# A tuned one-core transformer layer on Trainium2: 512 more columns of the projection in the opening sweep, a first softmax that stays unscaled, and modulation rows dealt out later

## The reference, cut to what matters

```python
ada = jax.nn.silu(c) @ w_ada[i] + b_ada[i]
sh_m, sc_m, gt_m, sh_f, sc_f, gt_f = [a[:, None, :] for a in jnp.split(ada, 6, axis=-1)]
h = rms_norm(x, g_pre_mix[i]) * (1 + sc_m) + sh_m
...
proj = h @ w_in
qa, ka, va, qb, kb, vb, rb, zb = jnp.split(proj, IN_SPLITS, axis=-1)
...
    p = jax.nn.softmax(s, axis=-1)
    pd = p[:, :, 0] - lam * p[:, :, 1]
    return jnp.einsum('bhqk,bhkd->bhqd', pd.astype(v.dtype), vt)
...
o = rms_norm(o, sub_gain) * (1.0 - lam_init)
```

## Time and profile before

| | |
|---|---|
| median of 3 runs | 1465.71 us (1464.82 to 1466.46) |
| the profiled execution | 1463.97 us, its span 1462.0 us |
| PE busy | 1221.2 us (84%) |
| DVE busy | 778.9 us (53%) |
| ACT, POOL busy | 211.7 us (14%), 52.9 us (4%) |
| DMA | 583.52 MB, mean 399 GB/s |

### The profile page before, as it was taken

The page is one execution under the profiler, slowest core; times in us unless marked ns, Lnnn a source line. Parts: engine busy times, 40 slices in busy tenths (PEclk is TensorE's granted clock), DMA queues, the critical chain, the costliest instruction groups (busy, mean ns, idle before and its releaser), DMA issues.

```text
span 1462.0 us, 18971 instructions
## 1 busy us (share of the span) xinstructions
PE 1221.2 (84%) x7437; PEld 575.1 (39%) x7438; DVE 778.9 (53%) x1110; ACT 211.7 (14%) x491; POOL 52.9 (4%) x68
## 2 busy tenths in 40 slices
PE   4699999999999989886777677758676679999967
PEld 4578884744444443222222222212222223333322
DVE  5877487877769666342234323422333335555525
ACT  3010121232110041010000000000000001111103
POOL 1000300011100020000000000000000000000020
PEclk9899999999999999988888889987888889999989
DMA  9999988797999899999999999999999999999996
GB/s 354 392 383 384 351 317 346 291 378 274 367 409 412 345 379 396 431 430 433 431 432 431 430 434 430 430 432 432 434 431 432 431 432 431 431 432 430 433 427 262
DMA packets 81557, 583.52 MB, mean 399 GB/s; under 512 B 5280, under 2 KB 30160, under 8 KB 56816
## 3 DMA queue, kind: packets, MB, share of 16 engines
q1 hardware_dynamic: 74160, 564.41, 93.6%
q10 hardware_dynamic: 5808, 14.85, 2.7%
q0 software_dynamic: 1552, 3.75, 0.8%
HBM read 579.30 MB, written 3.69 MB: 399 GB/s over the span
## 4 chain that ended last, share of the span: by engine, by line
PE 45%; DMA 44%; DVE 6%; SPq 2%; issue 1%; ACT 1%; POOL 0%; ACTq 0%; DVEq 0%
DMA stream<-in_w 41%; PE ps L1019 9%; PE ps L788 8%; PE ps L675 5%; PE ps L1075 4%; PE ps L740 3%; DMA stream<-in_w_ada 3%; PE ps L1026 2%; PE ps L975 2%; PE ps L878 2%; PE ps L969 2%; SPq L510 2%; PE ps L785 1%; DVE stream L1298 1%; DVE wk L1161 1%; DVE acc L1270 1%
## 5 line engine op out<-in xcount | busy, mean ns | idle before, releaser
L1019 PE MATMUL ps<-stream,wk 128*32 128x512 f32 x2304 | 330.2, 711 | 179.6 <-DMA stream<-in_w 178.9
L1536 DVE TENSOR_TENSOR acc<-ps,acc 128x2048 f32<-128x2048 f32 x37 | 84.8, 2292 | 364.4 <-PE ps L975 364.4
L1019 PEld LDWEIGHTS ps<-stream,wk 128*32 128x32 f32 x2304 | 74.7, 125 | 417.5 <-issue 332.5
L788 PE MATMUL ps<-stream 128*128 128x512 f32 x320 | 140.5, 593 | 0.1
L1075 PE MATMUL ps<-stream,cst 128*32 128x512 f32 x1152 | 131.5, 595 | 8.4 <-DMA stream<-in_w 8.4
L675 PE MATMUL ps<-stream 128*128 128x256 f32 x512 | 118.1, 394 | 1.8 <-ACT stream L1681 1.8
L675 PEld LDWEIGHTS ps<-stream 128*128 128x128 f32 x512 | 100.9, 198 | 16.8 <-issue 1.9
L1026 PEld LDWEIGHTS ps<-cst,wk 128*128 128x128 f32 x576 | 76.4, 207 | 69.0 <-issue 69.0
L975 PE MATMUL ps<-wk,cst 32*128 32x512 f32 x592 | 91.1, 687 | 0.8 <-ACT wk L1876 0.8
L1161 DVE SCALAR_TENSOR_TENSOR wk<-stream,cc,wk 128x768 f32<-128x768 f32 (+1 forms) x90 | 83.6, 929 | 11.0 <-DMA stream<-in_w_ada 8.3
L788 PEld LDWEIGHTS ps<-stream 128*128 128x128 f32 x320 | 59.5, 190 | 69.7 <-issue 69.7
(11 more groups left out here) (281 smaller groups left out, 1105.4 us busy)
## 6 DMA issues: line engine op xcount, KB each, us to landing
stream<-in_w SPq DMA_DIRECT2D x87, 4096.0 KB, 41.9
stream<-in_w_ada SPq DMA_DIRECT2D x64, 1024.0 KB, 8.8
stream<-in_w_in SPq DMA_DIRECT2D x8, 4096.0 KB, 16.5
stream<-in_w SPq DMA_DIRECT2D x16, 2048.0 KB, 11.7
stream<-in_w_ada SPq DMA_DIRECT2D x64, 384.0 KB, 10.1
stream<-in_w_ada SPq DMA_DIRECT2D x16, 512.0 KB, 9.7
stream<-in_w_in SPq DMA_DIRECT2D x4, 2048.0 KB, 13.7
stream<-in_w_out SPq DMA_DIRECT2D x2, 4096.0 KB, 16.4
```

The source lines that it names most:

```text
L788: last = nc.tensor.matmul(bank(fill % 2), hT[:, k, P * half:P * half + P], w[:, k, :], start=(k == 0), stop=(k == KD - 1))
L1019: last = nc.tensor.matmul(bank(1 + m)[32 * g:32 * g + 32, :], xe[:, k + g, :], w13[m][:, k + g, :], start=(k == 0), stop=(k == KD - 4))
L1536: V.tensor_tensor(y4, ps[:, b0:b0 + 4, :], y4, ALU.add).then_inc(ysum_sb, 1)
```

## The change

- **The opening sweep takes ten units.** `WIDE = 10`: units 8 and 9 are new. Each is the product of one tile of 128 positions with columns 2048 to 2559 of w_in (the first half of va), one matmul of 512 columns for each of the stage's rows. Their weights come as further slabs (`wide_slabs`, `wide_home`, L545 of the changed kernel), 2 KB a partition and row, 4.2 MB in all. Both share bank 6 with units 6 and 7, so there are four hand-overs of that bank in a stage where there were two (`SHARED = 4`, and `ADDED_AT` for their places on DVE; the fourth stands behind the stage's transposition and sum). `TURN = [6, 0, 7, 1, 8, 2, 3, 4, 9, 5]`.
- **The projection has 28 slots.** Block unit 4 is gone with its load, its 56 matmuls and its DVE sums; unit 5 is the only seven-product block. Plain projection starts in slot 4, attention too (`ATT_FROM = 4`).
- **`ADA_IN` is new.** In the last eight slots of the projection stand 18 of the 64 rows (3, 3, 3, 2, 1, 2, 2, 2 after an empty slot), where 16 stood in the last ten; two rows fewer (14) beside w_out.
- **The relative bias row** (L711 before) moves ahead of the sweep's last unit and into bank 7; its two tables are loaded on a semaphore of their own.
- **The first softmax stays unscaled.** L1414 is gone, and L1412 inverts one number in place of two. The two maps are combined as p0 + (l0/l1)(-lam) p1, where l0 and l1 are the softmax sums, and the RMS norm behind it absorbs the missing factor: POOL adds EPS * 128 * l0^2 to the sum of squares before the power. That adds two small operations a group of four steps on POOL ahead of its wait for the squares, and changes no count behind it.

The diff, cut to its core:

```diff
-HEADS_READY = [8, 16]
 EARLY = 8
+WIDE = 10
+SHARED = WIDE - 6
 HELD = 6
-TURN = [6, 0, 1, 2, 7, 3, 4, 5]
-SLOTS = 32
-BLOCK_UNITS = [4, 5]
+TURN = [6, 0, 7, 1, 8, 2, 3, 4, 9, 5]
+ADDED_AT = {8: {1: 6, 3: 7, 5: 8}, 4: {0: 6, 2: 7, 3: 8}}
+SLOTS = 28
+BLOCK_UNITS = [5]
-ATT_FROM = 6
-ADA_IN = [1, 1, 1, 1, 1, 1, 1, 1, 2, 2, 2, 2, 0, 2, 2, 1, 2, 2, 2, 1, 2, 2, 0, 2, 1, 2, 2, 2, 3, 2, 2, 0, 4, 5, 4, 3]
+ATT_FROM = 4
+ADA_IN = [1, 1, 1, 1, 2, 2, 2, 2, 2, 2, 0, 2, 2, 2, 2, 2, 2, 2, 2, 0, 3, 3, 3, 2, 1, 2, 2, 2, 4, 4, 3, 3]
...
+                for a_, b_ in wide_slabs(j):
+                    if a_ == 6:
+                        sp.wait_ge(xT_ps, 4 * TT)
+                    sp.dma_start(wide_home(a_, b_), w_in[:, a_:b_, 256 * EARLY:256 * EARLY + 512]).then_inc(early_w_in[j % 3], 16)
...
                 if not held and j + u > HELD:
-                    pe.wait_ge(add_sb, 2 * j + u - HELD)
+                    pe.wait_ge(add_sb, SHARED * j + u - HELD)
+                if u >= EARLY:
+                    t = u - EARLY
+                    for k in range(lo, hi):
+                        last = nc.tensor.matmul(bank(HELD), hT[:, k, P * t:P * t + P], wide_home(k, k + 1)[:, 0, :], start=(k == lo), stop=(k == hi - 1))
+                    last.then_inc(add_ps, 1)
+                    return last
...
+                    if n == WIDE - 1 and j + 1 == len(STAGES):
+                        pe.wait_ge(tab_in, 16 * len(tables))
+                        pe.wait_ge(early_mod, len(STAGES))
+                        nc.tensor.matmul(bank(7)[:, 0:SKEW], relb, bkt[:, 0:SKEW], start=True, stop=True).then_inc(relrow_ps, 1)
...
-                    if j and n_ in (len(pieces(j)) // 4, 3 * len(pieces(j)) // 4):
-                        added(j - 1, HELD + n_ // (len(pieces(j)) // 2))
+                    if j and n_ in ADDED_AT[len(pieces(j))]:
+                        added(j - 1, ADDED_AT[len(pieces(j))][n_])
...
+                if j:
+                    added(j - 1, WIDE - 1)
...
-                        link(V.reciprocal(st[:, 12:14], st[:, 10:12]))
-                        link(V.tensor_tensor(st[:, 14:15], st[:, 13:14], lamv[:, 5:6], ALU.mult))
-                        link(V.tensor_scalar(pr[:, 0, 0:nk], pr[:, 0, 0:nk], st[:, 12:13], None, ALU.mult))
+                        link(V.reciprocal(st[:, 13:14], st[:, 11:12]))
+                        link(V.scalar_tensor_tensor(out=st[:, 14:15], in0=st[:, 13:14], scalar=lamv[:, 5:6], in1=st[:, L0(i):L0(i) + 1], op0=ALU.mult, op1=ALU.mult))
...
+                    least = st[:, L0(4 * g):L0(4 * g) + 4]
+                    pool.wait_ge(p_exp, 4 * g + 4)
+                    pool.wait_ge(pd_sb, 4 * g + 4)
+                    link(nc.gpsimd.tensor_tensor(least, least, least, ALU.mult))
+                    link(nc.gpsimd.tensor_scalar(least, least, EPS * A_DV, None, ALU.mult))
                     pool.wait_ge(o_sq, g + 1)
```

More of the change, by code:

```diff
@@ L104, in slabs, with wide_slabs, slab_count, unit_landed @@
     return [(a, b) for a, b in ((lo, cut), (cut, hi)) if a < b]
+def wide_slabs(j):
+    lo, hi = STAGES[j]
+    cuts = [lo] + [k for k in range(lo + 1, hi) if k % HOMES in (0, 6)] + [hi]
+    return list(zip(cuts, cuts[1:]))
+def slab_count(j):
+    return len(slabs(j)) + len(wide_slabs(j))
+def unit_landed(v):
+    return 16 * ((v + 1) // 2)
 def slot_unit(s):
-    return 4 + s // 4, s // 2 % 2, s % 2
+    return 5 + s // 4, s // 2 % 2, s % 2
 def ada_slot(n):
@@ L153, in schedule @@
     beside = [[] for _ in range(SLOTS)]
-    beside[0] += [("alpha", 0), ("row",)]
+    beside[0] += [("alpha", 0)]
     beside[1] += [("alpha", 1)]
@@ L168, in schedule @@
         beside[ATT_FROM + j].append(("att", j))
-    beside[12].append(("kdec",))
-    beside[25].append(("kv", 0))
-    beside[26] += [("glao", 0), ("kv", 1)]
-    beside[27] += [("glao", 1), ("gsq", 0)]
-    beside[28] += [("gsq", 1)]
-    beside[29] += [("gmul", 0, 0), ("gmul", 1, 0)]
-    beside[30] += [("gmul", 0, 1)]
-    beside[31] += [("glaT", 0)]
+    beside[8].append(("kdec",))
+    beside[23].append(("kv", 0))
+    beside[24] += [("glao", 0), ("kv", 1)]
+    beside[25] += [("glao", 1), ("gsq", 0)]
+    beside[26] += [("gsq", 1), ("gmul", 0, 0)]
+    beside[27] += [("gmul", 1, 0), ("gmul", 0, 1), ("glaT", 0)]
     out = []
@@ L179, in schedule @@
         i, half, part = slot_unit(s)
-        out.append(("block", i - 4, 2 * half + part) if i in BLOCK_UNITS else ("proj", i, half, part))
+        out.append(("block", i - 5, 2 * half + part) if i in BLOCK_UNITS else ("proj", i, half, part))
         out += beside[s]
@@ L198, in loads @@
 def loads():
-    out = [(4 * i + 3.9, ("unit", i + 2)) for i in range(8)]
+    out = [(4 * i + 3.9, ("unit", i + 3)) for i in range(7)]
     out += [(max(ada_slot(n - 4) + 0.5, 1.9), ("ada", n)) for n in range(4, 64)]
-    return [("unit", 0), ("unit", 1), ("ada", 0), ("ada", 1), ("ada", 2), ("ada", 3)] + [item for _, item in sorted(out)]
+    return [("unit", 1), ("unit", 2), ("ada", 0), ("ada", 1), ("ada", 2), ("ada", 3)] + [item for _, item in sorted(out)]
 def build(nc, a, out):
@@ L683, in _ @@
             for j in range(len(STAGES)):
-                pe.wait_ge(early_w_in[j % 3], 16 * sum(len(slabs(i)) for i in range(j % 3, j + 1, 3)))
+                pe.wait_ge(early_w_in[j % 3], 16 * sum(slab_count(i) for i in range(j % 3, j + 1, 3)))
                 for n, u in enumerate(TURN):
-                    if n == EARLY - 2 and j + 1 < len(STAGES):
+                    if n == WIDE - 2 and j + 1 < len(STAGES):
                         early_sums(j + 1)
+                    if n == WIDE - 1 and j + 1 == len(STAGES):
+                        pe.wait_ge(tab_in, 16 * len(tables))
+                        pe.wait_ge(early_mod, len(STAGES))
+                        nc.tensor.matmul(bank(7)[:, 0:SKEW], relb, bkt[:, 0:SKEW], start=True, stop=True).then_inc(relrow_ps, 1)
                     last = early_unit(j, u)
@@ L709, in _ @@
                     fold(mod_bank(m)[:, 16 * m:16 * m + 16], 64).then_inc(mod_ps, 1)
-                elif kind == "row":
-                    nc.tensor.matmul(bank(4)[:, 0:SKEW], relb, bkt[:, 0:SKEW], start=True, stop=True).then_inc(relrow_ps, 1)
                 elif kind == "alpha":
@@ L1197, in _ @@
                 early(j)
-            for u in range(HELD, EARLY):
+            for u in range(HELD, WIDE - 1):
                 added(len(STAGES) - 1, u)
@@ L1684, in _ @@
             for u in range(HELD):
+                if u == HELD - 1:
+                    act.wait_ge(relrow_ps, 1)
+                    A(relrow, bank(7)[:, 0:SKEW], ACT.Copy).then_inc(relrow_sb, 1)
                 act.wait_ge(proj_ps, u + 1)
@@ L1702, in _ @@
                 kind = item[0]
-                if kind == "row":
-                    act.wait_ge(relrow_ps, 1)
-                    A(relrow, bank(4)[:, 0:SKEW], ACT.Copy).then_inc(relrow_sb, 1)
-                elif kind == "lam":
+                if kind == "lam":
                     act.wait_ge(lam_sum, 1)
@@ L1935, in _ @@
             pool.wait_ge(padded, 3)
+            for dst, src in tables:
+                pool.dma_start(dst, src).then_inc(tab_in, 16)
             for dst, src in params:
```

98 lines of the change are left out of this document (53 added, 45 removed).

## The result

| | before | changed |
|---|---|---|
| median of four runs each | 1466.09 us (1464.82 to 1467.61) | 1453.89 us (1452.07 to 1455.32) |
| ratio | | 0.9921, 95% interval 0.9909 to 0.9934 |
| profiled execution, span | 1463.97, 1462.0 us | 1453.37, 1451.5 us |

The change takes 12 us off the median and 10.5 off the span. Forecast were 1455.7, a range of 1450 to 1466, and a shorter time with a chance of 0.75.

The account below looks back on a forecast made before the run. The prediction took transfers to bound the kernel up to 125 us, then PE up to the experts, whose weight stream is fixed. Sweep +17.0, block -24.5, slots -1.5 and w_out -1.0 gave -10.0 us: 1455.7 against the median, range 1450 to 1466.

Parts of the forecast that it names:

- The sweep, +17.0: Opening sweep: ends 15.5 us later though 27.5 us of matmuls are added, plus 1.5 for the bank four units share.
- 2.8 us of low clock: Sweep, behind the first long wait of PE: the low clock stays and costs 2.8 us up to the next fold.
- the bias row: Moved from behind the first block part into the sweep: priced at 0, as PE works without a break in both.
- The shared bank, +1.5: Sweep: PE's wait for the bank that four units share, taken as 1.5 us between 0 and 8 in four stages.
- the rival that multiplied it by four stages: Sweep: PE waits 2.5 us a stage for the shared bank, using up the gain; 1470 at 3.5 us; chance 0.13.
- That PE and transfers would be level: Sweep stages from the second fold: PE 26.4 us, transfers 26.1, so waits and low clock at the folds go.
- The block, -24.5: Block products: 56 matmuls of 256 columns go, taking 24.5 us off PE, which works without a break there.
- The slots, -1.5: Plain projection slots: most of the 1.76 us stall goes, -1.5 us, between -1.8 and +2.
- w_out, -1.0: w_out's third block: two rows fewer beside w_out shorten PE's 2.98 us wait by 1.0, between 0 and 3.0.
- Sum: -10.0: Whole kernel: 17.0 - 24.5 - 1.5 - 1.0 = -10.0 us.
- The fourth rival: Whole kernel: all stalls go and the bank costs nothing, -14.3 us, 1451.5; chance 0.05.
- The last slots: Last eight projection slots: rows land in time, price 0; the rival says they run out, 1460, chance 0.14.

Follow-up runs that it names:

- e3: The changed kernel with the first softmax scaled again, as before the change: 1456.91 us, 0.9942 of the kernel before.
- e6: The changed kernel with DVE handing over bank 6 to units 6, 7 and 8 later: 1457.48 us, 0.9939 of the kernel before.
- e1: The changed kernel with the sweep's 32 added matmuls cut from 512 to 8 columns, loads kept: 1449.99 us, 0.989 of the kernel before.
- e2: The changed kernel without the 4.2 MB loads of the added columns, the matmuls reading other columns: 1450.59 us, 0.9897 of the kernel before.
- e11: The changed kernel without the loads of the added columns and with their matmuls at 8 columns: 1443.44 us, 0.9848 of the kernel before.
- e7: The kernel before with two modulation rows moved from w_out into the projection's last slot: 1467.54 us, 1.0009 of the kernel before.
- e9: The kernel before with two rows of w_ada issued earlier, ahead of the first w_out block: 1463.78 us, 0.9983 of the kernel before.
- e4: The changed kernel with two modulation rows moved from the last slot back beside w_out: 1454.14 us, 0.9915 of the kernel before.

## Why the prediction was right, and where its steps were off

- **The sweep, +17.0: +17.25 measured.** The sum was right, its pieces less so. The folds stand at 51.38, 78.73, 104.98, 131.22 and 158.40, forecast 51.2, 78.7, 105.1, 131.5 and 157.9. The second one is right by two errors against each other: 2.8 us of low clock were carried over from before, which did not come, and 2.08 of wait for the hand-over came instead. That is not only luck. In e3 the low clock did come behind a wait of 3.83 us (0.50 from 51.4 to 53.4), the wait for the hand-over was shorter for it, and the next fold stands at 78.53:

```profile
51.15 0.29 PE L681 MATMUL ps<-sums,cst 128*32 128x6 f32 x8 [3.83 <-DVE sums L1209]
62.72 5.45 PE L711 MATMUL ps<-stream 128*128 128x256 f32 x24 [0.91 <-DVE stream L1182]
```

  In these two DVE's hand-over sets the point, whatever the clock ahead of it was; in the changed kernel it ends at 62.87, having waited 0.91 us for a piece. The prediction has the low clock behind two waits of the kernel before, but it stood behind three (at 49.21, 74.23 and 99.41). Behind the last fold 24.2 us were measured against 22.9; 0.9 of it is the bias row, priced at 0 in both places. It costs 0.9 in the sweep and gives 0.9 back in the block.
- **The shared bank, +1.5:** 2.08 and 0.67 us, mis-sized by 1.25. One wait stands behind the fold at 51.38 and one behind that at 131.22, not two in each stage. e6 shows why the rival that multiplied it by four stages was wrong: once PE has been held up it runs behind DVE and isn't held up again.
- **That PE and transfers would be level, 26.4 against 26.1 us a stage,** is the step that carried the gain; e1, e2 and e11 show it. 27.5 us of matmuls and 0.9 of the bias row went in, 17.25 came out; 11 were done in time that had been idle or at low clock. The Trainium skill, page "DMA: Bandwidth & Descriptors", section "Where 436 GB/s comes from", would have had 358 GB/s and, by an estimate, 28.5 us a stage; the sweep ran at 382 to 392 from 60 to 140 us and the stages at 26.2 to 27.4, so the measurement decides against it here. The prediction's remark that the traces stand above 358 everywhere is wrong, though: slices of 274 to 354 stand in the earlier trace rows.
- **The block, -24.5: -24.5,** and another -0.9 for the bias row.
- **The slots, -1.5: -0.25.** This term was sized wrong, by 1.25. The stall of 1.76 us shrank to 0.13, but a new one of 0.90 stands at 336.93, where there was none. The reason given, that DVE would have room, was half the truth: e3 shows that without the shorter softmax these slots would have taken some 3.5 us more than before. The edit priced at "about 5 us, all of it beside PE" held the gain up rather than added to it.
- **w_out, -1.0: -3.2** up to the third block, and another -0.3 in the routing behind it, a size again, and in the other direction. The wait of 2.98 went altogether. The 5 us of traffic that I had worked out were more than the wait, and there was no reason to take a third. The place was wrong as well: e7 and e9 show that it matters which rows go ahead of the first w_out block, not how many slots beside w_out hold.
- **Sum: -10.0, with -11.8 at the first expert,** and 1.3 us back in the experts: -10.5 in the span. The sum is better than its terms: the sweep and the slots brought 1.5 us less than forecast, the block, w_out and the routing 3.3 more, and the experts' 1.3 had no term. That these partly cancel is luck. The fourth rival's -14.3 is a slip as well; its terms add up to -13.8 (15.5 - 24.5 - 1.8 - 3.0).
- **The last slots** did not run out of rows: glaT at 410.86 has no wait, as said.

## What to carry to other kernels

Where two resources are level, taking work off one brings little, and off both brings more than the sum (0.3 and 3.2, together 10.2 us): test them together. An edit is worth what the state of the kernel around it makes of it; the unscaled softmax was worth 0 alone and 3 us beside the other edits. For a transfer that is waited for, count all the bytes issued in the stretch without a pause, in queue order, and move a load out of that stretch. Moving two rows inside it brought nothing in e7 and made the block 4.4 us later in e4.
